# The lead-in of two PEER layers by half tiles, with the second head's work in layer 0 moved behind the first combinations

## What is computed

```python
x = layer_norm(ALPHA * x + g1 * mixer(x * (1 + sc1) + sh1))
x = layer_norm(ALPHA * x + g2 * peer_ffn(x * (1 + sc2) + sh2, wq, k1, k2, u_tab, v_tab))

def peer_ffn(t, wq, k1, k2, u_tab, v_tab):            # t (256, 1024)
    q = (t @ wq).reshape(256, 8, 256)                 # 8 heads
    v1, i1 = top_k(q[..., :128] @ k1.T, 16)           # 128 keys per half
    v2, i2 = top_k(q[..., 128:] @ k2.T, 16)
    top_s, pos = top_k((v1[..., :, None] + v2[..., None, :]).reshape(256, 8, 256), 16)
    idx = (i1 * 128 + i2) at pos                      # 16 experts per head and token
    g = softmax(top_s)
    act = gelu(einsum('td,thkd->thk', t, u_tab[idx]))
    return einsum('thk,thkd->td', g * act, v_tab[idx])
```

## Time and profile before

| | us |
|---|---|
| runs, median of 3 (lowest, highest) | 1882.37 (1879.37, 1882.44) |
| the profiled execution | 1878.28 |
| its span, first to last instruction | 1876.5 |
| TensorE busy, share of the span | 1666.7 (89%) |
| VectorE busy | 1465.8 (78%) |
| ScalarE busy | 600.9 (32%) |
| GpSimd busy | 482.8 (26%) |
| chain that ended last: TensorE, DMA, VectorE | 34%, 25%, 20% |
| moved by all DMA queues | 664.33 MB |

### The profile page before, as it was taken

One profiled execution on the slowest core, in us unless ns is written; L12 is line 12 of the kernel. 1 busy time (PEld: TensorE's weight loads), 2 busy tenths in 40 slices (PEclk: granted clock), 3 DMA queues, 4 the chain that ended last, 5 costly groups with the idle time before them and its releaser, 6 DMA issues.

```text
span 1876.5 us, 18237 instructions
## 1 busy us (share of the span) xinstructions
PE 1666.7 (89%) x5432; PEld 911.5 (49%) x5432; DVE 1465.8 (78%) x3511; ACT 600.9 (32%) x1493; POOL 482.8 (26%) x517
## 2 busy tenths in 40 slices
PE   8998999989989988889899999979999878877786
PEld 3787588545544433334333777545444423332332
DVE  6898975787678778988887799787787778777755
ACT  4665753223222223333322111032222323222221
POOL 0000000033333333333343000033333333333341
PEclk9999999999999999999999999989999999899999
DMA  8332139889999999999999685499999999999996
GB/s 358 135 135 96 68 119 403 329 311 412 426 418 427 427 425 414 391 425 427 417 419 427 261 311 226 193 413 426 427 426 423 426 422 419 423 416 427 420 421 271
DMA packets 95847, 664.33 MB, mean 354 GB/s; under 512 B 11358, under 2 KB 13375, under 8 KB 16389
## 3 DMA queue, kind: packets, MB, share of 16 engines
q0 software_dynamic: 73728, 536.90, 68.7%
q1 hardware_dynamic: 22020, 126.27, 17.3%
HBM read 662.02 MB, written 1.11 MB: 353 GB/s over the span
## 4 chain that ended last, share of the span: by engine, by line
PE 34%; DMA 25%; DVE 20%; issue 4%; ACT 2%; PEld 1%; DVEq 0%; PEldq 0%; POOL 0%; POOLq 0%
DMA expert_rows<-in_p_uv,chosen_experts 24%; PE bank L1169 20%; DVE dot_products L2454 7%; PE bank L1127 3%; PE bank L957 3%; PE bank L1029 2%; DVE silu_c_row_and_products L1866 1%; PE bank L1380 1%; ACT weight_diagonal L1706 1%; PEld bank L1169 1%; PE bank L1068 1%; DMA weight_block<-in_m_in_blocks 1%; PE bank L1283 1%; PE bank L1199 1%; PE bank L1206 1%
## 5 line engine op out<-in xcount | busy, mean ns | idle before, releaser
L1169 PE MATMUL bank<-expert_rows,weight_diagonal 128*128 128x512 f32 x2048 | 965.4, 616 | 162.4 <-ACT weight_diagonal L1706 162.0
L1420 POOL DMA_INDIRECT expert_rows<-in_p_uv,chosen_experts x512 | 482.4, 942 | 1367.0 <-PE bank L1169 776.3
L2454 DVE SCALAR_TENSOR_TENSOR dot_products<-expert_rows,bank 128x1024 f32<-128x1024 f32 x512 | 624.9, 1220 | 241.6 <-DMA expert_rows<-in_p_uv,chosen_experts 227.5
L1169 PEld LDWEIGHTS bank<-expert_rows,weight_diagonal 128*128 128x128 f32 x2048 | 382.5, 195 | 675.5 <-issue 391.6
L1706 ACT ACTIVATE weight_diagonal<-constants,expert_weights 128x128 f32<-128x128 f32 x512 | 177.8, 394 | 247.3 <-DVE expert_weights L2386 241.4
L1698 ACT ACTIVATE expert_gelu<-expert_dots 128x2 f32<-128x2 f32 x258 | 52.3, 203 | 614.1 <-DVE dot_products L2454 613.8
L917 PE MATMUL bank<-mixer_input_T_hi,weights_hi 128*128 128x512 f32 (+1 forms) x192 | 74.1, 386 | 8.4 <-DVE weights_lo L627 4.9
L2051 DVE SCALAR_TENSOR_TENSOR conv_work_or_state<-conv_work_or_state,channel_vectors 128x252 f32<-128x252 f32 (+2 forms) x192 | 71.8, 427 | 1.3 <-ACT conv_work_or_state L1529 1.0
L917 PE MATMUL bank<-mixer_input_T_lo,weights_hi 128*128 128x512 f32 (+1 forms) x192 | 72.2, 376 | 0.0
L917 PE MATMUL bank<-mixer_input_T_hi,weights_lo 128*128 128x512 f32 (+1 forms) x192 | 72.1, 376 | 0.0
L1299 PE MATMUL bank<-hyena_input_T,hyena_weight_block 128*128 128x256 f32 x320 | 70.5, 379 | 0.0
(11 more groups left out here) (324 smaller groups left out, 1899.4 us busy)
## 6 DMA issues: line engine op xcount, KB each, us to landing
weight_block<-in_ada_rows SPq DMA_DIRECT2D x24, 1024.0 KB, 7.1
weight_block<-in_m_in_blocks SPq DMA_DIRECT2D x20, 1024.0 KB, 6.6
hyena_weight_block<-in_ada_rows SPq DMA_DIRECT2D x15, 1024.0 KB, 7.1
hyena_weight_block<-in_h_in_blocks SPq DMA_DIRECT2D x12, 1024.0 KB, 6.9
weight_block<-in_wq_blocks SPq DMA_DIRECT2D x11, 1024.0 KB, 7.9
expert_rows<-in_p_uv,chosen_experts POOLq DMA_INDIRECT x512, 11.5
out_weights<-in_m_out_blocks SPq DMA_DIRECT2D x6, 1024.0 KB, 9.6
weight_block<-in_ada_shift SPq DMA_DIRECT2D x4, 1024.0 KB, 10.6
```

The costliest lines, as they stand in the source:

```text
L1169: last = mm(ps[b][:, :], dg[n % DIAG][:, :], uv[slot][:, D + h * 512:D + (h + 1) * 512], start=(r == 0 and k == 0), stop=end)
L1420: pool.indirect_dma_start(uv[slot][:, :], None, A[f"p_uv{l}"], bass.IndirectOffsetOnAxis(ap=chosen[:, s_, k:k + 1], axis=0)).then_inc(uv_l ...
L2454: stt(prod[:, :], uv[slot][:, 0:D], 1.0, rows_t, ALU.mult, ALU.mult, accum_out=dots[:, s_, k + j:k + j + 1]).then_inc(sem("dots_done"), 1)
```

## The change

It does the following, in both layers unless one is named.

- The last three blocks of tile 0's projection are done for the left half first and then for the right half, and VectorE works off the left half at once.
- The norm is applied in two halves of 512 channels with a signal each, TensorE transposes each half when it is there, and ScalarE modulates the second bank while VectorE does the first. For tile 1 ScalarE modulates both banks.
- Tile 0's chain stands ahead of all but five steps of tile 1's projection (`first_head`), with `token_rows` between the scores.
- `choose_first` reads the scores from PSUM, without ScalarE's copies.
- Two modulation dots of layer 1 (`LATE_DOTS`) move behind tile 0's modulation in layer 0.
- Layer 0: the second head's queries stand behind units 0 and 1, its scores and tile 1's transposes behind units 2 and 3; VectorE's pieces of that choice go from turns 0 to 4 to turns 2 to 4.
- Layer 1: `gate_rows`, the second head's queries and scores stand behind tile 1's projection, tile 1's norm on VectorE behind turn 0, its transposes on TensorE behind units 0 and 1. The slots begin at 6, so that gathers 0 and 1 need not wait for the projection.
- SP: the filter constants are loaded ahead of query block 3, which with query block 5 now waits for the two late dots.

The diff, cut to its core:

```diff
+FIRST_SLOT = (0, UVR - 2)
+LATE_DOTS = 2
...
-        return n, n % UVR, 16 * (n // UVR + 1)
+        return n, (n + FIRST_SLOT[l]) % UVR, 16 * (n // UVR + 1)
...
+        out_steps = [(k, h) for k in range(INNER // P) for h in range(2)]
+        out_steps_first = out_steps[:-6] + [(k, h) for h in range(2) for k in range(INNER // P - 3, INNER // P)]
...
-            pe.wait_ge(sem("layer_norms_done"), TT * 2 * l + t + 1)
             for j in range(2):
+                pe.wait_ge(sem("norm_halves"), 2 * (TT * l + t) + j + 1)
                 b = begin(("tT", l, t, j))
...
-            if l:
-                token_rows(1, 0)
-                tile_transposes(l, 1)
...
                     if l == 0 and s_ == 0 and k == 2:
-                        tile_transposes(0, 1)
+                        for c in range(2):
+                            second_queries(0, 0, c, 0, KD)
+                    if l == 0 and s_ == 0 and k == 4:
+                        second_scores(0, 0)
+                    if s_ == 0 and k == (4, 2)[l]:
+                        tile_transposes(l, 1)
                     combine(s_, k)
...
-                    chunks = ((4, 6, 8, 10), (2, 5, 8, 11))[l] if s_ == 0 else (0, 1, 2, 3)
+                    chunks = (4, 6, 8, 10) if s_ == 0 else (0, 1, 2, 3)
...
-        mixer_out(1, 0, 2)
-        tile_transposes(0, 0)
-        mixer_out(1, 2, 4)
-        first_queries(0, 0, 0, 0, KD)
-        first_queries(0, 0, 1, 0, 4)
-        first_half_scores(0, 0)
-        first_queries(0, 0, 1, 4, KD)
-        mixer_out(1, 4, 5)
-        first_half_scores(0, 1)
-        token_rows(0, 0)
-        mixer_out(1, 5, 8)
-        for c in range(2):
-            second_queries(0, 0, c, 0, KD)
-        mixer_out(1, 8, 10)
-        second_scores(0, 0)
-        mixer_out(1, 10, INNER // P)
+        def first_head(l, out_, steps):
+
+            out_(1, steps[0:4])
+            tile_transposes(l, 0)
+            out_(1, steps[4:5])
+            first_queries(l, 0, 0, 0, KD)
+            first_queries(l, 0, 1, 0, 4)
+            first_half_scores(l, 0)
+            first_queries(l, 0, 1, 4, KD)
+            token_rows(l, 0, (0,))
+            first_half_scores(l, 1)
+            token_rows(l, 0, (1,))
+
+        first_head(0, mixer_out, out_steps)
+        mixer_out(1, out_steps[5:])
         peer(0)
...
+        hyena_out(0, hyena_steps_first)
+        first_head(1, hyena_out, hyena_steps)
+        hyena_out(1, hyena_steps[5:])
         gate_rows(1, 1)
...
                         pool.wait_ge(sem("combined"), n - UVR + 1)
+                        if n == UNITS + UVR - FIRST_SLOT[1]:
+                            wait_full(pool, ("hout", 3))
...
         phase_end(pool, 1)
-        wait_full(pool, ("hout", 3))
         peer(1)
...
+            modulate_half(0, 1)
             copy_first_half(0)
-            copy_first_half_scores(0)
             copy_first_half(1)
-            copy_first_half_scores(1)
-            copy_second_queries(0)
-            copy_second_scores(0)
             gate_exp(0)
             if l:
-                ln_root(l, 0, 1)
+                gate_copy(1, 1)
+            if l:
+                copy_second_queries(0)
+                copy_second_scores(0)
...
+                    if s_ == 0 and k == (2, 0)[l]:
+                        ln_root(l, 0, 1)
+                    if l == 0 and s_ == 0 and k == 0:
+                        copy_second_queries(0)
+                    if l == 0 and s_ == 0 and k == 2:
+                        copy_second_scores(0)
+                    if s_ == 0 and k == (4, 2)[l]:
+                        for j in range(2):
+                            modulate_half(1, j)
...
-        for m in range(KD, 2 * KD):
+        for m in range(KD, 2 * KD - LATE_DOTS):
             modulation_dot(1, m)
...
-            modulate_tile(("tT", l), tT, l, 1, 0)
+            modulate_tile(("tT", l), tT, l, 1, 0, (0,))
+            if l == 0:
+                for m in range(2 * KD - LATE_DOTS, 2 * KD):
+                    modulation_dot(1, m)
...
-                modulate_tile(("tT", l), tT, l, 1, 1)
...
-            if l:
-                second_tile()
...
-                        for piece in ((0, 1), (2, 3), (4,), (5,), (6, 7))[n]:
+                        for piece in ((), (), (0, 1, 2, 3), (4, 5), (6, 7))[n]:
                             choose(1, piece)
...
-                    if l == 0 and s_ == 0 and k == 2:
+                    if s_ == 0 and k == (2, 0)[l]:
                         second_tile()
```

More of the change, by code:

```diff
@@ L377, in plan_peer @@
         work_, sums = (2, 0) if l else (0, 2)
-        for t in range(TT):
+        for t in range(TT - l):
             for j in range(2):
@@ L383, in plan_peer @@
             plan.use(("sc0", l, 0, c), 2 + c)
+        if l:
+            for h in range(2):
+                plan.use(("gate", 1, 1, h), 2 + h)
         for r in range(1, PH):
             tiled = () if l or r not in BY_TILE else (0,)
-            plan.use(("q1", l, 0) if r == 1 else ("q", l, r, *tiled), 3 if r == 1 else work_ + r % 2)
+            plan.use(("q1", l, 0) if r == 1 else ("q", l, r, *tiled), (6, 3)[l] if r == 1 else work_ + r % 2)
             plan.use(("sc1", l, 0) if r == 1 else ("sc", l, r, *tiled), 6 + r % 2)
+            if l and r == 1:
+                for j in range(2):
+                    plan.use(("tT", l, 1, j), 6 + j)
             if l == 0 and r == 3:
@@ L487, in build_in @@
     plan_inv(1, 1)
-    for h in range(2):
-        plan.use(("gate", 1, 1, h), 2 + h)
     for j in range(4):
@@ L1105, in second_scores, with token_rows @@
             last.then_inc(full[b], 1)
-        def token_rows(l, t):
-            for h in range(2):
+        def token_rows(l, t, halves_=(0, 1)):
+            for h in halves_:
                 b = begin(("tn", l, t, h))
@@ L1891, in gate_diagonal, with modulate_tile @@
                ada[l][:, GATES[j], :].unsqueeze(2).to_broadcast([P, KD, P]), ALU.mult).then_inc(sem("gate_diagonals"), 1)
-        def modulate_tile(key, dsts, l, pair, t):
-            for j in range(2):
+        def modulate_tile(key, dsts, l, pair, t, banks_=(0, 1)):
+            for j in banks_:
                 b = wait_full(dve, key + (t, j))
@@ L2344, in choose_first @@
             def choose_first():
-                for piece in (0, 2, 1, 3):
-                    a = piece % 2
-                    if piece < 2:
-                        wait_read(dve, ("sc0", l, 0, a))
-                    after(best(topv[:, a, :], topi[:, a, :], sc[:, 0, 0, a, :], left[:, a, :], piece >= 2))
+                for a in range(2):
+                    b = wait_full(dve, ("sc0", l, 0, a))
+                    scored = ps[b][:, a * P:(a + 1) * P]
+                    after(step(V.max(topv[:, a, 0:8], scored)))
+                    step(V.max_index(topi[:, a, 0:8], topv[:, a, 0:8], scored))
+                    V.match_replace(left[:, a, :], topv[:, a, 0:8], scored, LOWEST).then_inc(read[b], 1)
+                    wait_read(dve, ("sc0", l, 0, a))
+                    after(best(topv[:, a, :], topi[:, a, :], None, left[:, a, :], True))
                 choose(0, 4)
```

109 lines of the change are left out of this document (57 added, 52 removed).

## The result

The changed kernel takes 1887.12 us in the median of seven runs (1884.03 to 1889.19), the kernel before 1881.98 on the same chip (1876.48 to 1883.07). The ratio is **1.0034, 95% interval 1.0023 to 1.0045: slower, by 4.3 to 8.5 us**. The forecast said no change. The profiled executions differ by 5.9 us (spans 1882.4 and 1876.5), and the first reading is where these come from.

The account below looks back on a forecast made before the run. The end was taken to be set by the last moment a gather stream's DMA waits for a gather's issue. Layer 0 +2.4 and layer 1 -2.2 gave +0.2 us, forecast as a 1882.5 us median, range 1876 to 1888.

Parts of the forecast that it names:

- Layer 0's lead-in: Layer 0, tile 0's chain to the first gather: gather at 375.3, 5.5 us earlier; tile 1's projection ends at 392.8.
- Layer 0, what is given back: Layer 0, second queries' copy delays the gelu of units 2 and 3; gather 17 at 430.2, layer 0 2.4 us late.
- Layer 1's lead-in: Layer 1, the same chain to the first gather: gather at 1210.3, 5.4 us earlier.
- Layer 1, unit 0: Layer 1, first combination: unit 0 combined at 1222.9 instead of 1231.31.
- TensorE's row of work is then 2.2 earlier and stays so up to gather 28: Layer 1, from unit 8 to gather 28: TensorE's lead holds, so the layer gains 2.2 us; bounds 3.9 and 0.
- The other bound of the term, 0: Layer 1's gain of 2.2 us was bounded by 3.9, what the queue alone would allow, and 0.
- The sum: Whole kernel: +2.4 - 2.2 = +0.2 us on the profiled 1878.28, giving 1878.5; 1882.5 as the median of runs.
- The condition that I had set: Sign of error: the gap between the layers' last units differs from before by more than 4 us.
- The chances of the three outcomes: Whole kernel: faster 0.18, same 0.63, slower 0.19, from forecast 0.62, rivals 0.12, 0.06, 0.16, and 0.04 unseen.
- The clock: Rival, both layers: idle gaps ahead of early units lower TensorE's clock, +5.2 us in all, 1887.5; chance 0.16.
- The early gathers of layer 1: Rival, layer 1: the two early gathers still leave behind the projection, 3.5 us later; 1883.1, no chance of its own.
- The two rules: Trainium skill: 1.38 us drain per ScalarE table load, set aside for the rows; TensorE idle-gap warning, taken as the clock rival.

Follow-up runs that it names:

- l0_free: The changed kernel with layer 0's second-head queries and scores copied behind the gelu and diagonals of units 2 and 3; ratio to the kernel before 0.9995.
- l1_copy12: The changed kernel with layer 1's copies of the third head's queries and scores back behind units 12 and 14; ratio to the kernel before 1.0010.
- warm: The changed kernel with unread products added to keep TensorE busy in the idle gaps of both layers' first units; ratio to the kernel before 1.0038.
- norm_first: The kernel with both copy-order mends, plus layer 1's tile 1 norm ahead of turn 0 in VectorE's idle time; ratio to the kernel before 0.9939.
- l0_back: The changed kernel with layer 0's second head back within tile 1's projection, its copies ahead of ScalarE's first exponential; ratio to the kernel before 0.9999.
- `both`: The changed kernel with layer 0 as in l0_free and layer 1 as in l1_copy12; ratio to the kernel before 0.9973.
- pad6: `both` with six one-column copies added to ScalarE's program in the Hyena stage; one run, 1871.92 us against 1882.36 for the kernel before.
- pad24: `both` with 24 one-column copies added to ScalarE's program in the Hyena stage; one run, 1871.76 us against 1882.36 for the kernel before.
- gate_behind: norm_first with layer 1's gate rows and their copies behind the second head's, its queries in bank 6 instead of 3; ratio to the kernel before 0.9939.

## Why the prediction was wrong, step by step

- **Layer 0's lead-in: right.** Gather 0 at 375.46 (375.3), transposes at 362.23 (362.3), queries at 364.44 (364.45), tile 1's projection to 392.8 (392.8). This part came out term by term.
- **Layer 0, what is given back: right.** Weights at 400.49 (400.6), unit 4 at 412.85 (413.2), unit 8 at 423.91 (424.5), gather 17 at 429.67 (430.2). The term was +2.4; it is +1.85 at gather 17, and 0.63 at the last gather of the layer, a difference within the spread of that stretch. l0_free shows that the named cause is the cause.
- **Layer 1's lead-in: right.** Gather 0 is 4.6 earlier, and 5.0 against the layer's own start, which is 0.42 late (5.4 was forecast).
- **Layer 1, unit 0: too early by 3.5.** I had 1222.9, it was 1226.37. Of that 0.42 is the layer's late start, 0.78 a wait of the second queries for the gate copies, which share bank 3 with them (I had not followed that these now stand right ahead), and 1.50 the wait without a name. The other 0.8 is small terms: the gate rows took 1.88 and the second queries 3.81, where I had 1.7 and 3.46. Behind unit 0 the forecast held up to unit 8, which started 25.4 us behind unit 0 (1251.74; forecast 25.6). So gather 16, which waits for unit 8, left 0.66 later than before, where I had unit 8 2.2 earlier, and against layer 0's last gather it is 0.03 later: the lead of this term was gone before the step that failed next.
- **The step that failed: "TensorE's row of work is then 2.2 earlier and stays so up to gather 28".** The diff moves ScalarE's copy of the third head's queries in layer 1 from behind unit 12 to behind unit 10, ahead of the exponential's and the gelu's table loads. I costed the choice's pieces at these turns and never this copy, so the sum puts it at nothing, without a reason. VectorE waits 8.08 us for the gelu of units 12 and 13, and putting the copies back gives 4.5 us of the whole (l1_copy12). The term was -2.2 and is +4.5 at gather 28 (b): 2.2 of the miss is the late unit 0, 4.5 is this. The other bound of the term, 0, was therefore no bound: it held only for an edit in which nothing behind unit 8 changes.
- **The sum.** Forecast +2.4 - 2.2 = +0.2. Measured on the two traces: +0.6 at layer 0's last gather, +5.3 in layer 1, together 5.9. The condition that I had set (the gap between the layers' last units differs by more than 4) is met, with 5.29 between the last gathers. The chances of the three outcomes don't quite follow from their parts either: the parts give about 0.19 faster, 0.63 same and 0.17 slower, where I wrote 0.18, 0.63 and 0.19.
- **The rivals.** The clock gave the right side and nearly the right time (1887.5) by luck, for a wrong reason: with the clock kept up in the gaps that it named the kernel is no faster (warm), and with more of the low clock but the copies back in place it is (l1_copy12). The early gathers of layer 1 did leave early.
- **The two rules.** After the change too the load at 1261.24 takes 1.28 and its exponential starts at 1262.53. The drain that the Trainium skill adds ("ScalarE: Activation LUTs", section "What ACT_TABLE_LOAD costs") doesn't show here. The granted clock was 0.50 in 410 to 415, in the gap ahead of unit 4 of layer 0, and warm shows that this costs nothing there, since VectorE sets the pace. So the trace agrees with the warning of the Trainium skill ("TensorE: Matmul & The Clock Gate", section "Why this matters for your kernels") that idle gaps lower the clock, but its price in time is nothing at these units.

## What to carry to other kernels

The rows of one engine run in the order of its program: a gelu that was ready at 391.1 ran at 400.26, behind a copy that waited. So a step that waits for another engine belongs behind everything that is ready: copies of queries and scores, moved by one turn (two units) along ScalarE's program, were worth 7 us in one layer and 4.5 in the other. When a diff moves a step, list for every engine it touches what now stands behind it and when that was ready, at the small moves too; the one that I skipped was a change from 12 to 10. An earlier start of a stream counts only if its eight slots come free in time: look at the last late unit, fill an engine's idle time ahead of it (norm_first), and expect the gain there.

## What the runs showed of the hardware

- In the change TensorE's granted clock was 0.50 (1.2 GHz) over 410 to 415, in and behind an idle gap of 5.73 us (layer 0), and 0.66 over 1235 to 1240, behind one of 4.09. With products put into these gaps it stayed at 1.00 (2.4 GHz) there. A unit behind such a gap took up to twice as long (3.78 us for 1.98), and the whole time didn't move. Behind a shorter gap of 2.8 us ahead of unit 12 of layer 1 it stayed at 1.00 in the change (2.81) and fell in warm (2.82), where gather 20 then left 1.4 us later behind unit 0.
- In layer 1, between the end of the second queries and their copy on ScalarE, time can pass in which neither engine shows work: 1.5 us in the change, 1.6 in l1_copy12, l0_back and `both`, 2.3 in l0_free, 3.0 in warm, 1.4 to 1.5 in pad6 and pad24. In the kernel before and in gate_behind it is 0.04, in norm_first 0.45. In each of the eight kernels with over 1 us a packet of instructions starts in this time, among the gathers' packets: 0.1 to 0.7 us ahead of the copy in seven, and two packets 1.6 and 1.2 us ahead of it in warm. In the other three none does. For the change, the queues in 1222.0 to 1222.5 (packets, MB, share of the time):

```profile
q0 software_dynamic: 30, 0.22, 112.7%
q14 instruction: 1, 0.01, 3.9%
```

So the wait goes together with the fetch of a piece of program over DMA engines that the gathers fill. But the packet takes 0.31 us (0.35 in `both`), and in five of the eight kernels (the change, l0_back, `both`, pad6, pad24) its record ends only after the copy has begun, by up to 0.25 us, which speaks against the fetch as what the copy waited for. Six or 24 instructions more on ScalarE change neither. Whose piece of program it is, and what the wait is for, stays open.
